# One of four channel tiles of a causal convolution, moved from VectorE to TensorE as products with diagonal matrices

## What is computed

```python
u = p_conv[..., :512] * sigmoid(p_conv[..., 512:])
u = lax.conv_general_dilated(u, conv_w[:, None, :], window_strides=(1,),
        padding=[(30, 0)], feature_group_count=512, ...) + conv_b
y_conv = silu(layer_norm(u, conv_ln_g, conv_ln_b))
...
y_rw = rwkv7_scan(r, decay, k, v, kk, a)      # per head, token after token
y_rw = layer_norm(y_rw, eps=GN_EPS) * rw_lnx_g + rw_lnx_b
y_rw = (y_rw + bonus) * g
y1 = concatenate([y_conv, y_rw], axis=-1) @ w_out
```

## Time and profile before

| | |
|---|---|
| time, median of 3 runs | 3590.02 us (3589.89 to 3595.82) |
| profiled execution, its own time | 3595.08 us |
| span in the profile | 3593.8 us |
| mean granted clock | 0.951 |
| busy: PE, DVE, ACT, POOL | 91%, 63%, 40%, 47% |
| mixer of the second block, from the inversion's first level to the end of the convolution | 1974.8 to 2172.7 us |
| of this: five levels / products after / scan / end up to the last tap | 75.2 / 17.7 / 57.6 / 47.2 us |

### The profile page before, as it was taken

One profiled execution on the slowest core, in us unless ns is written; L12 is line 12 of the kernel. 1 busy time (PEld: TensorE's weight loads), 2 busy tenths in 40 slices (PEclk: granted clock), 3 DMA queues, 4 the chain that ended last, 5 costly groups with the idle time before them and its releaser, 6 DMA issues.

```text
span 3593.8 us, 47940 instructions
## 1 busy us (share of the span) xinstructions
PE 3258.5 (91%) x18421; PEld 2761.1 (77%) x18421; DVE 2261.1 (63%) x3832; ACT 1437.7 (40%) x2272; POOL 1707.0 (47%) x930
## 2 busy tenths in 40 slices
PE   6996788999999888999898867899999999999997
PEld 6886676888777666888576754699999998888885
DVE  4176547555544556542457677256998995887885
ACT  4554434222433434232353422433333674333333
POOL 5742323444322213444332211347888544888883
PEclk9998899999999999999998968999999999999998
DMA  5520213344322212432221000237899898999993
GB/s 187 179 74 24 82 59 105 129 141 141 116 77 65 71 36 81 154 117 94 91 71 42 3 25 24 82 118 265 304 322 324 271 315 301 379 352 357 349 352 126
DMA packets 303698, 575.31 MB, mean 160 GB/s; under 512 B 13296, under 2 KB 224240, under 8 KB 287088
## 3 DMA queue, kind: packets, MB, share of 16 engines
q1 hardware_dynamic: 251824, 369.13, 30.5%
q0 software_dynamic: 42432, 152.78, 11.8%
q10 hardware_dynamic: 9216, 50.34, 3.7%
HBM read 515.57 MB, written 56.62 MB: 159 GB/s over the span
## 4 chain that ended last, share of the span: by engine, by line
PE 75%; DVE 13%; issue 5%; ACT 4%; POOL 3%; DMA 1%; POOLq 0%; DVEq 0%; SPq 0%; ACTq 0%
PE bank L464 18%; PE bank L466 18%; PE bank L465 18%; PE twin L464 3%; PE twin L466 3%; PE twin L465 3%; PE bank L2789 2%; POOL split_low L450 2%; PE bank L545 2%; DVE arena_rw L2261 2%; PE bank L1791 1%; PE bank L1767 1%; DVE branch L588 1%; PE bank L2065 1%; DVE residual L638 1%
## 5 line engine op out<-in xcount | busy, mean ns | idle before, releaser
L450 POOL TENSOR_TENSOR split_low<-weights,split_high 128x1024 fp32r<-128x1024 f32 x554 | 1354.7, 2451 | 1575.0 <-ACT split_high L442 1571.2
L464 PE MATMUL bank<-normed_high,split_high 128*128 128x384 f32 (+1 forms) x1992 | 735.7, 369 | 43.5 <-issue 23.3
L465 PE MATMUL bank<-normed_low,split_high 128*128 128x384 f32 (+1 forms) x1992 | 725.5, 364 | 0.0
L466 PE MATMUL bank<-normed_high,split_low 128*128 128x384 f32 (+1 forms) x1992 | 725.1, 364 | 0.0
L442 ACT CAST split_high<-weights 128x1024 fp32r<-128x1024 f32 x554 | 571.2, 1046 | 362.5 <-PE bank L466 205.6
L464 PEld LDWEIGHTS bank<-normed_high,split_high 128*128 128x128 f32 x1992 | 378.7, 190 | 90.6 <-issue 47.4
L465 PEld LDWEIGHTS bank<-normed_low,split_high 128*128 128x128 f32 x1992 | 378.8, 190 | 40.1 <-issue 2.0
L466 PEld LDWEIGHTS bank<-normed_high,split_low 128*128 128x128 f32 x1992 | 377.9, 190 | 40.2
L464 PE MATMUL bank<-split_high,wide_hidden_high 128*128 128x512 f32 x768 | 300.7, 392 | 10.8 <-DVE wide_hidden_low L3004 6.0
L465 PE MATMUL bank<-split_low,wide_hidden_high 128*128 128x512 f32 x768 | 300.2, 391 | 0.0
L466 PE MATMUL bank<-split_high,wide_hidden_low 128*128 128x512 f32 x768 | 300.1, 391 | 0.0
(11 more groups left out here) (627 smaller groups left out, 6449.5 us busy)
## 6 DMA issues: line engine op xcount, KB each, us to landing
weights<-in_w_ff SPq DMA_DIRECT2D x64, 1024.0 KB, 5.4
weights<-in_peer_u SPq DMA_DIRECT2D x64, 1024.0 KB, 7.2
weights<-in_peer_v SPq DMA_DIRECT2D x64, 1024.0 KB, 8.9
weights<-in_cond_w SPq DMA_DIRECT2D x24, 1024.0 KB, 6.8
early_table<-branch SPq DMA_DIRECT2D x128, 192.0 KB, 4.6
gate_table<-arena SPq DMA_DIRECT2D x12, 2048.0 KB, 10.4
lates<-early_table ACTq DMA_DIRECT2D x32, 768.0 KB, 9.8
gates<-gate_table ACTq DMA_DIRECT2D x32, 768.0 KB, 12.7
```

The costliest lines, as they stand in the source:

```text
L450: pool.do.tensor_tensor(lo, raw_unit(u), hi.bitcast(F32), ALU.subtract).then_inc(*pool.sig("split_low", u))
L464: pe.do.matmul(o, ah, bh, start=first, stop=False)
L465: pe.do.matmul(o, ah, bl, start=False, stop=False)
L466: return pe.do.matmul(o, al, bh, start=False, stop=last)
```

## The change

Tile 3 of the convolution leaves `dve_conv`, which has 93 steps now. `pe_conv` does its 31 taps as products: for each tap a 128x128 diagonal matrix of that tap's weights is the stationary operand, and the 512 tokens of `r_pad` at the tap's shift stream through it, in fp32, all into one bank, which is held from the first tap to the last. The matrices come from DRAM (prepared ahead by the host as a layout of the weights, 2 loads of 1 MB, 16 taps in the first and 15 in the second), through the list of weight loads, between the last chunk of `w_in` and the first of `w_out`. PE's program takes one tap after each `inv_a`, two after each `a_turned` in step 3, one after each of the first two product groups of a scan chunk and two at its end; after 20 + 8 + 3 of them it has none left, so that the last is at the end of chunk 0. There ACT adds the bias and copies the bank to the convolution's tile 3 (`act_conv`). DVE's calls of `conv_some` are as before.

```diff
+CONV_PE = (3,)
+CONV_LOADS = 2 * len(CONV_PE)
+CONV_TAPS = 16
...
+        conv_first = loads.index(("chunk", W["R", "ab"][-1])) + 1
+        loads[conv_first:conv_first] = [("conv", j) for j in range(CONV_LOADS)]
...
+                    elif was == "conv":
+                        sp.wait_ge(at("conv_part", j))
...
+                elif kind == "conv":
+                    source = dram["conv_diagonals"][i]
...
+        def pe_conv():
+            for i, c in enumerate(CONV_PE):
+                bank, empty = banks.take("conv", c)
+                pe.wait_ge(empty, at("conv_in", c), at("conv_pad"))
+                for tap in range(CONV_K):
+                    j, at_tap = 2 * i + tap // CONV_TAPS, tap % CONV_TAPS
+                    pe.wait_ge(landed("conv", j))
+                    last = pe.do.matmul(bank, raw_tile("conv", j)[:, at_tap * P:(at_tap + 1) * P],
+                                        r_pad[:, c, tap:tap + T], start=tap == 0, stop=tap == CONV_K - 1)
+                    if at_tap == CONV_TAPS - 1 or tap == CONV_K - 1:
+                        last.then_inc(*pe.sig("conv_part", j))
+                    if tap == CONV_K - 1:
+                        banks.give(("conv", c), ("conv_kept", c))
+                    yield
...
         def dve_conv():
             for tap in range(CONV_K):
-                for c in range(4):
+                for c in sorted(set(range(4)) - set(CONV_PE)):
...
+            taps = pe_conv()
...
                     pe_small_products(("inv_a", lv, c), tmp[c], plain(X[:, c, :]), [at("inv_masked", lv, c), x_at(lv, c)],
                                       [("inv_a_kept", lv, c)])
+                    conv_some(taps, 1)
...
                 pe_turns(("a_turned", c), a_hat[:, c, :], None, [("a_turned_kept", c)])
+                conv_some(taps, 2)
...
             for ch in range(N_CH):
-                pe_scan(ch)
+                pe_scan(ch, taps)
+            run(taps)
...
                 banks.give(("scan_u", ch, hh), ("scan_uu", ch, hh))
+            conv_some(taps, 1)
...
             banks.give(("scan_gain", ch), ("scan_sum", ch))
+            conv_some(taps, 1)
...
             banks.give(("scan_new", ch), ("rw_out", ch))
+            conv_some(taps, 2)
...
+        def act_conv(c):
+            act.wait_ge(at("conv_part", 2 * CONV_PE.index(c) + 1))
+            act.do.activation(conv[:, c, :], banks.tile("conv", c), ACT.Identity, bias=col("conv_b_2", c)
+                              ).then_inc(*act.sig("conv_kept", c))
...
+                if ch == 0:
+                    act_conv(CONV_PE[0])
```

More of the change, by code:

```diff
@@ L123 @@
                    "rw_before rw_bonus rw_gated rw_k rw_lw rw_out rw_rk rw_shifted rw_total scan_state scan_sum scan_uu",
-    "act_rw_done": "rw_cur b_tok conv_gate conv_sigmoid inv_a_kept inv_kept_act k_tok kk_norm mv_kept n_kept rw_a rw_before_exp "
+    "act_rw_done": "conv_kept rw_cur b_tok conv_gate conv_sigmoid inv_a_kept inv_kept_act k_tok kk_norm mv_kept n_kept rw_a rw_before_exp "
                    "rw_gate rw_gd rw_inverse_exp rw_lw_sigmoid rw_out_old rw_p rw_total_exp rw_wd v_tok ya_kept ymv_kept",
-    "pe_rw_done": "a_turned b_turned gram gram_n inv_a inv_b k_turned lora_a lora_g lora_w mv scan_gain scan_new scan_old "
+    "pe_rw_done": "conv_part a_turned b_turned gram gram_n inv_a inv_b k_turned lora_a lora_g lora_w mv scan_gain scan_new scan_old "
                   "scan_u v_turned x_turned y_turned ya ymv",
@@ L2343, in pe_rw @@
                 banks.give(("lora_g", c), ("rw_gated", c))
-            pe_center("conv-", 4, conv_mean, lambda i: conv[:, i, :], lambda i: at("conv_tap", CONV_K - 1, i),
+            pe_center("conv-", 4, conv_mean, lambda i: conv[:, i, :], lambda i: at("conv_kept", i) if i in CONV_PE else at("conv_tap", CONV_K - 1, i),
                       [("conv_centered", 3)])
@@ L2369, in scan_heads, with pe_scan @@
                     slice((hh * TT + tk) * 64, (hh * TT + tk) * 64 + 64)
-        def pe_scan(ch):
+        def pe_scan(ch, taps):
             part, tk, tsl, old, new, uu = scan_slices(ch)
@@ L2444, in act_rw @@
                             ).then_inc(*act.sig("rw_out_old", ch))
+                if ch == 0:
+                    act_conv(CONV_PE[0])
             meet(act, "act", "rw_scanned")
+            for c in CONV_PE[1:]:
+                act_conv(c)
             act_split(2 * W["R", "o"][0] + AHEAD)
@@ L3246, in layouts @@
     dist = np.clip(p_ + T - P - u_, -REL_CLIP, REL_CLIP) + REL_CLIP
+    taps = a["conv_w_2"].reshape(CONV_K, 4, P)
+    diagonals = np.zeros((CONV_LOADS, P, CONV_TAPS, P), np.float32)
+    for i, c in enumerate(CONV_PE):
+        for tap in range(CONV_K):
+            diagonals[2 * i + tap // CONV_TAPS, range(P), tap % CONV_TAPS, range(P)] = taps[tap, c]
     out = {
+        "conv_diagonals": diagonals.reshape(CONV_LOADS, P, CHUNK_WORDS),
         "columns": np.concatenate(cols, axis=1),
```

## The result

| | before | changed |
|---|---|---|
| median | 3590.27 us (3587.22 to 3595.82) | 3597.51 us (3592.49 to 3604.26) |
| ratio to before | | 1.0018, 95% interval 1.0012 to 1.0024 |
| profiled execution, its own time and span | 3595.08, 3593.8 us | 3596.48, 3595.2 us |

Each median is of 20 executions. The changed kernel is 7.2 us slower by the medians, 6.5 by the ratio (4.3 to 8.6 by its interval). The forecast was 7.9 us. "Slower by over 0.2%" and "within 0.2%" had been given nearly the same chance, and the result lies on that line.

What follows compares the result with a forecast made beforehand. DVE's tap row bounds the mixer's end, PE the A halves of the levels. -22.7 + 23.4 (levels) + 5.6 (products after) + 1.6 (scan) = +7.9 us, so 3590.0 becomes 3597.9 us; range 3587 to 3606.

Steps and rivals of the forecast that it cites:

- DVE's row at the end: End of the mixer: DVE's row falls from 56 taps to 25, all on the path, -22.7 us.
- a change of more than 1 us behind the last tap: After DVE's last tap at the end: any change above 1 us was to show the prediction wrong.
- What is late next: End: 25 taps take 18.3 us, longer than the 16.65 us until ACT's last root, so nothing else becomes late.
- Taps in the levels: A halves of the inversion's levels: 20 taps on PE at 1.17 us each, all on the path, +23.4 us.
- Rival 2: Array shape changes around taps are free, 0.86 us a tap: +1.1, 3591.1 us; chance 0.24 together with rival 1 without the scan.
- rival 3: Levels: taps cause or meet more clock falls, five for three: +12 to +14 us, 3603; chance 0.16.
- Taps after the inversion: Products after the inversion: 8 taps, two behind each a_turned, partly covered by PE's wait for ACT, +5.6 us.
- Chunk 0: First scan chunk: three taps on PE, partly covered by its waits for DVE, +1.6 us together.
- The clock in the scan: Scan: PE's clock expected to stay down for most of it, as before; put at nothing.
- rival 1: Levels and perhaps scan: long streams keep PE's clock up; +2.6 us, or -8 with the scan (chance 0.07).
- Bank, loads, ACT: One ring bank fewer, diagonals loaded ahead of w_out, one more ACT activation in chunk 0: each put at nothing.
- rival 1 without the scan: Only the levels' three clock falls vanish, worth 5.1 us: +2.6, 3592.6 us; chance 0.24 together with Rival 2.

Runs made afterwards that it cites:

- experiment 6: Changed kernel with all 31 PE taps at the end, behind the gate's products, and ACT's bias and second w_out split later; ratio to before 0.9952.
- Experiment 3: Changed kernel with each of PE's 31 taps issued twice in a row, so tile 3's sum is doubled; ratio to before 1.0104.
- experiment 1: Changed kernel with a level's four taps in one group ahead of the first inv_a; 3588.78 us, ratio to before 0.9993.
- experiment 2: Changed kernel with only the first and last of PE's 31 taps done, the other 29 left out; ratio to before 0.9947.
- experiment 4: Changed kernel with PE's 31 taps moved to where PE waits: B halves, each scan chunk, the end; 3554.20 us, ratio to before 0.991.
- experiment 5: As experiment 4, but the taps of seven scan chunks moved to the end, one left in chunk 0; 3567.25 us, ratio to before 0.993.
- experiment 9: As experiment 8, but two PE taps in each scan chunk and none at the end; 3543.83 us, ratio to before 0.9865.
- experiment 8: As experiment 4, plus five of DVE's taps at each level's start, none left for the end; 3553.49 us, ratio to before 0.9899.

## Why the prediction was right

- **DVE's row at the end.** Expected -22.7; measured -20.5 to the first scaling, -21.8 to the end of the stretch. The term is mis-sized by the price of one tap. I had divided the whole row of 56 by 56 (0.733), but two taps at its start run beside POOL's splits (25 taps took 20.17 us in the changed kernel, 16.64 without POOL in experiment 6), and that loss stays with any row that begins there. A tap is 0.666, and 31 are 20.6. The row of 25 so took 20.17 us and not 18.3, and PE's wait was 12.8 and not near 10. The other 1.2 us came back behind the row, where the sums of the convolution's squares met a higher clock (5.09 us for 6.40). The prediction had named a change of more than 1 us behind the last tap as a sign of being wrong, and this is one, if a small one.
- **What is late next** (ACT's roots, 16.65 us): right, and 25 taps still outlast it.
- **Taps in the levels.** Expected +23.4 at 1.17 each; 1.20 each by the trace, 24.0, and the stage +26.7 (level 2 took 21.6 us, 21.1 had been expected). Experiment 3 shows that all 20 are on the path, experiment 1 that 0.34 of the 1.20 comes from the place between groups of 64x64 products. Rival 2 (free changes) falls. The rest, 2.7 us, goes with the clock: low for 17 us of the levels (four falls, one of twice the length) and not for 10. At half the speed the 7 us more cost up to 3.5. The 17 us are as long as the five falls of rival 3, so this rival was there as well; that the taps caused the falls is not shown, for in experiment 2, with one tap in the levels for 20, the clock is low for the same 17 us there.
- **Taps after the inversion.** Expected +5.6; +5.65.
- **Chunk 0.** Expected +1.6; 6.97 - 5.35 = +1.62.
- **The clock in the scan.** I put it at nothing. It fell in the third chunk instead of the second, and the scan without its +1.6 became 3.5 us shorter. This is rival 1 in small, and experiment 1, with the same three taps in chunk 0, is like it: the clock fell 20 us into the scan (16 in the changed kernel). In the eight kernels with fewer taps in chunk 0, the one before among them, it fell 0.2 to 6.9 us into the scan; in experiment 3, with the three taps doubled, at 1.8 us for 3.3 us, and for good at 18.8. So the delay probably comes from the three taps, as far as one execution of each kernel can tell; they are not enough to keep the clock up. That rival 1 had something to it experiments 4, 5 and 9 show, though the clock did not stay up there either: it fell and came back.
- **Bank, loads, ACT.** Put at nothing; experiment 2, which has them but for one late chunk, shows nothing above some 2 us for them.
- **Its own sums.** Two don't come out: rival 1 without the scan is 7.9 - 5.1 = +2.8, not +2.6, and rival 2 with one fall less is 3591.1 - 1.7 = 3589.4, not the 3587 at which the range began. Neither touches the forecast.

By the stages the misses are +0.9 at the end, +3.3 in the levels and -3.5 in the scan, together +0.7 (8.65 for 7.9); the medians moved by 7.2. They cancel, and that is luck: the mechanism and the prices of the taps were right, but the clock, put at nothing, moved the levels and the scan by about 3 us in opposite directions, which is also as much as a stage moves by itself (see experiment 6).

What stays open: what in PE's work the clock goes by. Experiments 8 and 4 have the same PE program and differ (0.69 and 0.89 in the scan). The taps in the chunks bring the clock back, but after how long is left open: 7, 10 and 34 us in three kernels.

## What to carry to other kernels

Two engines that hand the pace to each other each have a half in which work is free, and moving work to the other engine was worth nothing here until it stood in that engine's free half: with the 31 products in PE's half, levels, products and scan were 30.5 us longer than before; with them in its waits, 14.0 us shorter, by a higher clock. Before moving work to another engine, look whether the first one has idle time at another place: six of DVE's own taps in each level gave 20 us with nothing moved. And group products of one array shape together: a 128x512 product between 64x64 groups cost 0.34 us more than one behind its like.

## What the runs showed of the hardware that I had not expected

- TensorE's clock in a stage with many 64x64 products can be raised by giving it more to do. Scans with no or one 128x512 fp32 product in all took 57.6 to 61.0 us at 0.51 to 0.56; with three in chunk 0 55.8 and 54.9 at 0.64 and 0.68; with one in each chunk 55.1 and 47.6 at 0.69 and 0.89; with two in each 48.0 at 0.93.
- DVE's tap of 128x512 takes 0.67 us by itself, and two of them took 4.93 us beside POOL's splits in the changed kernel (that POOL is the cause is read from where its splits lie in experiment 6 and here; no run changed only that):

```profile
2156.43 4.93 DVE L2285 SCALAR_TENSOR_TENSOR arena_rw<-arena_rw,columns 128x512 f32<-128x512 f32 x2
```
